# The attention's last dilation: scores of three pairs and one turn among the value layer's phases, and two value products in a row behind it

## The reference

```python
proj = (u @ w_in).reshape(B, S, N_GROUPS, 3, ATT_HEADS, ATT_HEAD_DIM)
for gi, (window, dilation) in enumerate(DILATED_GROUPS):
    q = apply_partial_rope(proj[:, :, gi, 0], cos, sin) * scale
    k = apply_partial_rope(proj[:, :, gi, 1], cos, sin)
    v = proj[:, :, gi, 2]
    o_g, lse_g = dilated_group_attention(q, k, v, window, dilation)   # softmax(q k^T, masked) v, and log of its sum
wts = softmax(stack(lses), axis=0)
o = einsum('gbsh,gbshd->bshd', wts, stack(outs))
return o.reshape(B, S, D_MODEL) @ w_out
```

## Time and profile before

| | |
|---|---|
| median of 3 runs | 2596.79 us (2594.71 to 2598.24) |
| profiled execution | 2592.83 us, span 2591.0 us |
| TensorE busy | 96% of the span |
| VectorE busy | 52% |
| ScalarE busy | 22% |
| GpSimd busy | 6% |
| value layer and tail of group 2 | about 2273 to 2326 us of the span |

### The profile page before, as it was taken

One profiled execution on the slowest core, in us unless ns is written; L12 is line 12 of the kernel. 1 busy time (PEld: TensorE's weight loads), 2 busy tenths in 40 slices (PEclk: granted clock), 3 DMA queues, 4 the chain that ended last, 5 costly groups with the idle time before them and its releaser, 6 DMA issues.

```text
span 2591.0 us, 40918 instructions
## 1 busy us (share of the span) xinstructions
PE 2500.2 (96%) x17894; PEld 1998.7 (77%) x17894; DVE 1353.9 (52%) x1900; ACT 567.8 (22%) x931; POOL 157.5 (6%) x142
## 2 busy tenths in 40 slices
PE   8999999999999999999999999999999999989998
PEld 5787888999968788885333335958999978958998
DVE  4674322599467733222122112675599576674455
ACT  1163110110112721102222222231210211222111
POOL 0002220000000023100000000000000011000000
PEclk9999999999999999998999999999999999999999
DMA  7433123688444421116999997342688343433441
GB/s 262 163 131 114 60 72 114 227 334 322 154 146 147 147 98 66 66 53 214 357 371 343 365 359 251 114 153 93 223 335 312 116 163 132 156 103 122 169 158 73
DMA packets 229841, 476.42 MB, mean 184 GB/s; under 512 B 14240, under 2 KB 43552, under 8 KB 229408
## 3 DMA queue, kind: packets, MB, share of 16 engines
q1 hardware_dynamic: 229088, 472.28, 51.6%
q10 hardware_dynamic: 576, 1.52, 0.2%
HBM read 472.70 MB, written 1.05 MB: 183 GB/s over the span
## 4 chain that ended last, share of the span: by engine, by line
PE 86%; DVE 6%; DMA 3%; ACT 2%; issue 2%; SPq 1%; DVEq 0%; POOL 0%; ACTq 0%
PE ps L510 18%; PE ps L1807 16%; PE ps L583 12%; PE ps L2350 10%; PE ps L575 9%; PE ps L1985 7%; PE ps L1228 2%; PE ps L1239 2%; PE ps L1235 1%; SPq L3530 1%; PE ps L2316 1%; DMA ring<-in_exp_w_up 1%; PE ps L2649 1%; DVE work L1480 1%; DMA work<-in_exp_w_down 1%
## 5 line engine op out<-in xcount | busy, mean ns | idle before, releaser
L510 PE MATMUL ps<-xu,ring 128*128 128x256 f32 x1792 | 410.2, 386 | 22.3 <-DMA ring<-in_w_in 9.5
L510 PEld LDWEIGHTS ps<-xu,ring 128*128 128x128 f32 x1792 | 340.9, 194 | 69.5 <-issue 21.2
L583 PEld LDWEIGHTS ps<-xu,ring 128*128 128x128 f32 x2336 | 267.6, 194 | 7.4 <-issue 6.2
L583 PE MATMUL ps<-xu,ring 128*128 128x128 f32 x2336 | 269.8, 277 | 2.5 <-ACT xu L961 2.3
L1807 PE MATMUL ps<-xu,work 128*128 128x128 f32 x2112 | 238.8, 275 | 0.0
L1807 PEld LDWEIGHTS ps<-xu,work 128*128 128x128 f32 x2112 | 237.3, 192 | 0.0
L575 PE MATMUL ps<-ring,xu 128*128 128x512 f32 x520 | 227.6, 593 | 1.3 <-DVE ring L668 1.3
L2350 PE MATMUL ps<-ring,work 128*32 128x512 f32 (+1 forms) x1776 | 183.5, 562 | 8.5 <-ACT ring L2421 5.5
L575 PEld LDWEIGHTS ps<-ring,xu 128*128 128x128 f32 x520 | 97.8, 190 | 119.9 <-issue 115.7
L1807 PE MATMUL ps<-xu,ring 128*128 128x128 f32 x1584 | 181.4, 276 | 2.6 <-ACT xu L961 1.9
L1807 PEld LDWEIGHTS ps<-xu,ring 128*128 128x128 f32 x1584 | 179.0, 192 | 4.5 <-issue 3.7
(11 more groups left out here) (479 smaller groups left out, 3369.1 us busy)
## 6 DMA issues: line engine op xcount, KB each, us to landing
ring<-in_w_in SPq DMA_DIRECT2D x72, 1024.0 KB, 5.1
work<-in_ada_w SPq DMA_DIRECT2D x48, 1024.0 KB, 10.9
ring<-in_attn_w_in SPq DMA_DIRECT2D x36, 1024.0 KB, 5.2
ring<-in_ffn_w_in SPq DMA_DIRECT2D x32, 1024.0 KB, 7.5
ring<-in_exp_w_down SPq DMA_DIRECT2D x112, 256.0 KB, 4.9
ring<-in_exp_w_gate SPq DMA_DIRECT2D x88, 256.0 KB, 4.6
ring<-in_ffn_w_out SPq DMA_DIRECT2D x22, 1024.0 KB, 8.3
ring<-in_exp_w_up SPq DMA_DIRECT2D x80, 256.0 KB, 4.8
```

The source lines that it names most:

```text
L510: mm = pe.matmul(acc[:, m * T:(m + 1) * T], w[:, k, m * P:(m + 1) * P], src[:, half * 4 + k, :], start=(half == 0 and k == 0 and m % 2 == ...
L583: mm = pe.matmul(acc[:, m * P:(m + 1) * P], w[:, k, m * P:(m + 1) * P], x[:, k, :], start=(start and m == 0 and k == 0), stop=True, skip_g ...
```

## The change

Only the list of steps behind the phases of group 2's value layer changes. Scores 0 move from behind P5 to behind P2, scores 1 from behind P3 to behind P5, turn 0 from behind P7 to behind P3. Scores 2 follow P7, turn 1 follows, then scores 3, and then the value products 0 and 1 one after the other, turns 2 and 3, and products 2 and 3. The new list is: P4, P1, P2, s0, P5, s1, P6, P3, t0, P7, s2, t1, s3, o0, o1, t2, t3, o2, o3. No step is added or removed.

```diff
--- before.py
+++ after.py
@@ -3174,7 +3174,7 @@
                 order = ("P1", "P2", "P4") + PHASES[3:] if (g, which) == (0, 0) else PHASES
                 return [("ph", g, which, p) for p in order]
 
-            steps_ = [("s", 0), ("s", 1), ("t", 0), ("s", 2), ("t", 1), ("o", 0), ("s", 3), ("t", 2), ("o", 1), ("t", 3), ("o", 2), ("o", 3)]
+            last = [("t", 1), ("s", 3), ("o", 0), ("o", 1), ("t", 2), ("t", 3), ("o", 2), ("o", 3)]
             seq = phases(0, 0) + phases(0, 1) + phases(0, 2)
             beside = {0: {"P1": "s1", "P2": "t0", "P6": "s2 t1", "P3": "o0", "P7": "s3"},
                       1: {"P4": "t2", "P5": "o1", "P6": "t3", "P3": "o2", "P7": "o3"}}
@@ -3186,9 +3186,9 @@
                         seq += [(w[0], g, int(w[1]), None) for w in beside[which].get(step[3], "").split()]
                 for step in phases(g + 1, 2):
                     seq.append(step)
-                    if g == 1 and step[3] in ("P5", "P3"):
-                        seq.append(("s", 2, ("P5", "P3").index(step[3]), None))
-            return seq + [(w, 2, pr, None) for w, pr in steps_[2:]]
+                    if g == 1:
+                        seq += [(w[0], 2, int(w[1]), None) for w in {"P2": "s0", "P5": "s1", "P3": "t0", "P7": "s2"}.get(step[3], "").split()]
+            return seq + [(w, 2, pr, None) for w, pr in last]
 
         AT_SEQ = attention_order()
         at_sums = [area(16 + 0.5 * i, 512).rearrange("p (k t) -> p k t", t=P) for i in range(4)]
```

## The result

The changed kernel takes 2599.26 us (median of 19 runs, 2595.41 to 2604.66) against 2596.32 us of the kernel before (19 runs, 2590.78 to 2600.32). The ratio is 1.0016, 95% interval 1.0010 to 1.0022. So it is 2.9 us over before by the medians, forecast +2.8. The recorded ratio is not the quotient of the two medians; taken times 2596 us it makes the loss 4.2 us, with an interval from 2.6 to 5.7. Either way it is a small loss, clear of zero, and the ratio lies within the 0.2% that the prediction called no change. The profiled execution took 2596.44 us, span 2594.6.

What follows compares the result with a forecast made beforehand. The tail was taken as bounded by VectorE's unbroken row, not TensorE. Order +0.2, clock at P3 +2.1 and at L867 +0.5 sum to +2.8 us; with the step from profiled run to median, 2599.6 us, range 2594.5 to 2603.5.

Steps and rivals of the forecast that it cites:

- Scores 0: Behind P2, they run inside TensorE's 1.71 us hole ahead of P5: 1.31 us gained on TensorE, none on VectorE.
- The snapshot: ScalarE's copy of P5's bank falls behind pair 0's exponentials, so P3, which waits for it, starts 3.9 us later.
- Rival (c): Faster: P3 isn't held by the snapshot and starts at 2293.5; 2595.5 us, or 2592.5 with the projection at full clock; chance 0.06.
- Turn 0 and the weights: Turn 0 ahead of P7 lets VectorE's 3.25 us of pair 0 weights run beside P7; the later P7 (3.3) cancels it.
- The tail: From scores 2 to pair 2's output VectorE does the same blocks in another order, 17.5 us, with its row unbroken.
- DMA: SyncE's loads of the next projection: P3 frees the last slab 3.9 us later, covered by over 25 us.
- The clock: TensorE's clock falls once in the new 3.8 us hole ahead of P3, +2.1 us; larger hole ahead of L867, +0.5 us.
- the order's wash: Gains and losses on VectorE's row from the new order nearly cancel: +0.2 us at the projection's first turn, L867.
- rival (a): Wash with no fall of the clock that counts: +0.2 us, 2597.0 us; chance 0.20.
- rival (b): Slower by over 0.2%: the clock stays low over P3, turn 0, P7 and scores 2, 8.8 us, 2605.8 us; chance 0.12.
- The bound for no change: What a measurement of this kernel tells from no change, put at about 0.2%, 5.2 us; same was given 0.83.

Runs made afterwards that it cites:

- e1: Changed kernel with only ScalarE's queue put back: snapshots of P5 and P6 ahead of the exponentials of pairs 0 and 1; ratio to before 0.9990.
- e3: Changed kernel with only scores 0 and 1 moved; turn 0 stays behind P7 and the tail keeps its old order; ratio to before 1.0012.
- e5: Changed kernel with only turn 0 moved, ahead of P7; scores 0 and 1 and the tail in the old order; ratio to before 0.9993.
- e4: Changed kernel with only the new order behind the phases; scores 0 and 1 stand where they stood before; ratio to before 1.0006.
- e8: Changed kernel with 18 unread products of 128 columns filling TensorE's hole ahead of the projection's first turn (L867); ratio to before 0.9999.
- e6: Changed kernel with 36 unread products of 128 columns ahead of the projection's first turn (L867), overfilling that hole; ratio to before 1.0019.

## Why the prediction was right

**Scores 0.** Right: no gain beyond TensorE's hole. P5 and P6 stand where they stood.

**The snapshot.** Right, and it is the step that decides. Forecast: P3 starts 3.9 us later, behind a hole of 3.8 us, held by P5's snapshot behind pair 0's exponentials. Measured: 3.97 us later from P4 (24.48 against 20.51), with 3.81 us idle, ended by L648. e1 puts only ScalarE's order right and wins 5.4 us at the first L867. Rival (c), that something else holds P3, is gone. Its price of 1.3 us was too small: it left P7 waiting for P6's snapshot, where e1 moves that one too.

**Turn 0 and the weights.** Right. The block of 3.25 us left the row and lay beside P7 with 0.33 us to spare. e3, without it, ends 3.2 us later at the first L867 than the changed kernel. e5 shows that the turn's move alone is worth 0.9 us at scores 2, of which 0.2 is left at the first L867.

**The tail.** Right: 17.47 us in either order, and e4 finds its order alone worth nothing.

**DMA.** Right. SyncE's four loads end their issue at 2272.33 + 27.14 = 2299.47, against 2294.95 before, which is 4.1 us later with the late start taken off. The projection's own wait is 1.71 us as before.

**The clock.** Forecast +2.1 at P3 and +0.5 at L867. Measured in the one profile 5.37 - 3.60 = 1.77 and 1.94 - 1.06 = 0.88. With the order's wash of 0.2 (1.95 - 1.77) that makes 2.83 us at the start of the projection, forecast 2.8. The projection's first 32 were taken to cost what they did before, 9.90, and took 10.20; this 0.3 us is not in the sum. The sum also counted on a fall in the hole; in this profile the hole passed at full clock and the fall came 1.4 us into P3.

That it fits so closely is partly luck. Behind the same hole P3 took 3.67, 5.37 and 6.71 us in different executions, so rival (a), no fall at P3, and the beginning of rival (b), a longer one, each show in single executions of programs that don't differ up to there. The price of 2.1 at P3, a choice between 0.7 and 3.0, lies inside what came: 0.07, 1.77 and 3.11 over 3.60. The median over runs need not be the one of the profile. Rival (b) as a loss of 8.8 us was not seen.

**What the forecast left out.** The forecast left out that the order could have won: the sum called the order a wash without saying that the snapshot's place was a choice. With ScalarE's order put right the same moves of TensorE and VectorE win 3.4 us at the first L867.

**The bound for no change.** Some 0.2% was set as what a measurement could tell. With 19 runs of each the interval was a third as wide as that (0.06% to either side), so the loss of 0.16% could be told from zero.

## What to carry to other kernels

When one list orders several engines, walk each engine's queue through a change, those too that the change isn't about. Here moving TensorE's scores ahead also put ScalarE's copy, which the next phase waits for, behind exponentials that could not start yet; a copy that somebody waits for belongs ahead of work that waits itself. And a hole ahead of dense matmuls can cost its own length and some clock on top: count it at both levels, and try to fill it where the order can't close it, with no more than it holds. Here order and filling together beat the kernel before by 0.22%; a gain of the filling alone was not clear of the noise.

## What the runs showed of the hardware

The same hole of 3.81 us ahead of the same matmuls was followed by a P3 of 3.67, 5.37, 5.37 and 6.71 us in four programs that are alike up to there. The clock fell 1.4 us into P3 in the changed kernel, 0.7 us ahead of P3 in e8, and not at P3 in e6. What the granted clock does behind a hole of this length differs from execution to execution; a single profile doesn't give its price. A product of 128 columns in fp32 stood in the record as two matmuls, 0.11 us apart, so 16 of them take 3.6 us and 32 take 7.1. The same holds for the value phases: four products of 512 columns in the code are the eight matmuls of a phase in the record, 0.43 us apart. Whoever sizes a filling from a count of matmuls in a profile has to know this.
